# A streaming-encoder block on one core: rotation and decay masks moved from the chunk tiles into the input projection, through DRAM

## What is computed

```python
proj = x @ w_in                                   # one combined input projection
aq, ak = apply_rope(aq), apply_rope(ak)           # t1*c - t2*s, t2*c + t1*s
y_attn = banded_sink_attention(aq, ak, av, sinks) # chunks of 64 frames
g = cumsum(g)                                     # per chunk and head
decay = exp(where(tril, g[..., :, None] - g[..., None, :], -inf))
m_low = where(strict, einsum(k_beta, k) * decay, 0)
t_inv = solve(eye + m_low, eye)                   # then a scan over 16 chunks
o = (q * exp(g)) @ state + (q k^T * decay) @ v_new
```

## Time and profile before

| | us |
|---|---|
| median of 3 runs (lowest, highest) | 1432.07 (1429.08, 1433.17) |
| the profiled execution, its own time | 1435.67 |
| its span, first to last instruction | 1433.9 |
| input pairs, PE's first product to the first filler | 33.1 to 307.2 |
| chunk tiles, step -2 | 307.2 to 325.2 |
| chunk tiles, steps -1 to 7 | 325.2 to 620.2 |

### The profile page before, as it was taken

How to read it: one execution, slowest core, us unless ns; L and a number is a source line. 1 busy time by engine, 2 the same in 40 slices (tenths; PEclk the granted TensorE clock), 3 DMA queues, 4 the chain that set the end, 5 groups by cost and what they waited for, 6 DMA issues and landing times.

```text
span 1433.9 us, 22065 instructions
## 1 busy us (share of the span) xinstructions
PE 1392.7 (97%) x8430; PEld 1154.0 (80%) x8430; DVE 1024.1 (71%) x1860; ACT 600.7 (42%) x1300; POOL 257.4 (18%) x265
## 2 busy tenths in 40 slices
PE   9999999999999899999999999999999999999997
PEld 8788887877778778778888888888888888888885
DVE  7999863436888888754618798667665677777778
ACT  5555534321333333343202436554554544444540
POOL 4322222223332332514730000000000000000002
PEclk9999999999999999999999999999999999999998
DMA  6233322264244332123551234334444976555422
GB/s 209 89 117 118 117 105 102 105 197 107 77 119 106 84 105 66 62 105 132 176 206 59 88 133 158 134 143 160 162 161 144 347 235 182 167 166 183 126 73 117
DMA packets 114136, 195.01 MB, mean 136 GB/s; under 512 B 27696, under 2 KB 59632, under 8 KB 111728
## 3 DMA queue, kind: packets, MB, share of 16 engines
q1 hardware_dynamic: 105104, 174.21, 36.9%
q10 hardware_dynamic: 8928, 19.40, 3.5%
HBM read 135.84 MB, written 57.74 MB: 135 GB/s over the span
## 4 chain that ended last, share of the span: by engine, by line
PE 85%; DVE 11%; issue 1%; DMA 1%; ACT 1%; SPq 0%; ACTq 0%; DVEq 0%
PE ps L2498 6%; PE ps L2497 6%; PE ps L2496 6%; PE ps L2060 6%; PE ps L2479 6%; PE ps L2480 6%; PE ps L2481 6%; PE ps L2062 6%; PE ps L2061 6%; PE ps L2114 5%; PE ps L2000 4%; PE ps L2001 4%; PE ps L2002 4%; PE ps L2181 3%; PE ps L2373 2%; PE ps L2374 2%
## 5 line engine op out<-in xcount | busy, mean ns | idle before, releaser
L2497 PE MATMUL ps<-tlow,shi 128*128 128x512 f32 x416 | 162.0, 389 | 0.0
L2498 PE MATMUL ps<-thi,slow 128*128 128x512 f32 x416 | 162.0, 389 | 0.0
L2496 PE MATMUL ps<-thi,shi 128*128 128x512 f32 x416 | 162.0, 389 | 0.0
L886 POOL TENSOR_TENSOR zt<-zt,ln2gb 128x256 f32<-128x256 f32 x4 | 3.4, 852 | 691.6 <-ACT zt L1332 691.6
L896 ACT ACTIVATE thi<-b 128x512 fp32r<-128x512 f32 x104 | 65.5, 629 | 107.6 <-PE ps L2498 107.4
L1884 DVE TENSOR_TENSOR tlow<-b,thi 128x512 fp32r<-128x512 f32 x104 | 71.8, 691 | 52.7 <-ACT thi L896 52.6
L2497 PEld LDWEIGHTS ps<-tlow,shi 128*128 128x128 f32 x416 | 78.1, 188 | 16.3
L2496 PEld LDWEIGHTS ps<-thi,shi 128*128 128x128 f32 x416 | 78.1, 188 | 16.2
L2498 PEld LDWEIGHTS ps<-thi,slow 128*128 128x128 f32 x416 | 78.1, 188 | 16.1
L1877 DVE TENSOR_TENSOR slow<-sraw,shi 128x512 fp32r<-128x512 f32 x104 | 71.4, 687 | 21.6 <-ACT shi L896 21.1
L896 ACT ACTIVATE shi<-sraw 128x512 fp32r<-128x512 f32 x104 | 65.1, 626 | 32.8 <-DMA zt<-xpark 16.1
(11 more groups left out here) (444 smaller groups left out, 3940.5 us busy)
## 6 DMA issues: line engine op xcount, KB each, us to landing
raw<-in_wblk SPq DMA_DIRECT2D x55, 512.0 KB, 4.4
sraw<-hpark SPq DMA_DIRECT2D x104, 256.0 KB, 2.8
hpark<-hq SPq DMA_DIRECT2D x16, 1024.0 KB, 4.7
b<-in_wblk SPq DMA_DIRECT2D x64, 256.0 KB, 3.7
wraw<-in_wblk SPq DMA_DIRECT2D x30, 512.0 KB, 3.9
hpark<-hq SPq DMA_DIRECT2D x16, 768.0 KB, 5.0
park<-cb ACTq DMA_DIRECT2D x34, 256.0 KB, 2.5
park<-cacc ACTq DMA_DIRECT2D x12, 512.0 KB, 3.3
```

The costliest lines, as they stand in the source:

```text
L2496: mm(outp, shi[s][:, ts], thi[m][:, :], start=first, stop=False, skip_group_check=True)
L2497: mm(outp, shi[s][:, ts], tlow[m][:, :], start=False, stop=False, skip_group_check=True)
L2498: return mm(outp, slow[s][:, ts], thi[m][:, :], start=False, stop=final, skip_group_check=True)
```

## The change

- The rotation is done in the input pairs. Ten half rows (five blocks of `park` times two halves of 512 frames) pass one after the other through one buffer: ACT issues the loads (`rope_load`: one transfer of the block, four of the swapped quarters, at three of them a table), POOL does three operations of 128x512 (`rope`), SP stores the half row back. `rope_load(u)` waits for the store of `rope(u - 1)`. In the tiles SP loads the rotated values straight into `qb` and `kr`.
- The decays of all eight tiles are made in the input pairs from pair 8 on. Their rows go to DRAM (`gpark`); from pair 10 on ACT loads one tile's rows spread over 128 partitions (`dec_load`), DVE makes the arguments (`dec_args`), ACT the exponentials (`dec_exps`) and the store to `dpark`, again through one buffer. In each step SP loads the finished masks of a tile (`load_dec`). `a_grow`, `a_d`, `a_em`, `a_eg` and `a_exps` are gone; `a_trk` takes over the wait of `a_grow`.
- Six filler weight blocks are split by ACT (`split_hi`) and DVE (`split_lo`) instead of POOL.
- The orders of the steps are new on all engines, with 28 places for fillers; the number of fillers stays 384 (52 instead of 50 of them in step -2, 51 instead of 65 in step 7). Decay sums and rates move to pairs 7 to 9.

```diff
-    [0, 0, 6, 0, 1, 0, 0, 0, 0, 0, 0, 0, 0, 1, 0, 1, 0, 2, 2, 0, 0, 0, 13, 1, 2, 0, 0, 21, 0, 0, 0],
...
+    [7, 2, 0, 0, 0, 4, 6, 0, 0, 1, 1, 2, 0, 0, 0, 4, 0, 0, 0, 0, 0, 3, 0, 0, 22, 0, 0, 0],
...
+BEHIND = {-1: LATE + 2, 1: LATE + 3, 2: LATE + 4, 3: LATE + 5, 5: LATE + 6, 6: LATE + 7}
...
+        ROPE = [(0, 0), (1, 0), (2, 0), (0, 1), (1, 1), (2, 1), (3, 1), (4, 1), (3, 0), (4, 0)]
+        ROPE_TAB = [n for n, (_, h) in enumerate(ROPE) if n == 0 or ROPE[n - 1][1] != h]
+        ROPE0, DEC0 = 8, 10
+        ROPE_IN = [16 * (5 * (n + 1) + sum(m <= n for m in ROPE_TAB)) for n in range(len(ROPE))]
+        def rope_cols(n):
+            i, h = ROPE[n]
+            return B_Q + i, slice(PAD + h * HALF, PAD + (h + 1) * HALF)
...
+            def load_dec(t):
+                if t:
+                    sp.wait_ge(m_ok, 2 * t)
+                    sp.wait_ge(at_ok, t)
+                    sp.wait_ge(qegt_ok, t)
+                else:
+                    sp.wait_ge(dec_out, 16 * NT)
+                sp.dma_start(dec[:, :], dpark[t, :, :]).then_inc(dec_in, 16)
...
+                if t:
+                    sp.wait_ge(sc_mm, 2 * t)
+                else:
+                    sp.wait_ge(init_ok, 1)
+                    sp.wait_ge(rope_out, 16 * len(ROPE))
+                    sp.wait_ge(pad_out, 48)
+                for e, r in enumerate(chunks):
+                    for c in range(2):
+                        a = PAD + t * P + c * CH
+                        sp.dma_start(qb[r, c, :, r], park[B_Q:B_Q + N_Q, r, a:a + CH].rearrange("b p s -> p b s")).then_inc(bt_in, 16)
+                sp.dma_start(kr[:, :], park[B_K, :, t * P:t * P + 192]).then_inc(bt_in, 16)
...
+                for u in (2 * (n - ROPE0) - 3, 2 * (n - ROPE0) - 2):
+                    if 0 <= u < len(ROPE):
+                        sp.wait_ge(rope_ok, u + 1)
+                        b, sl = rope_cols(u)
+                        sp.dma_start(park[b, :, sl], rraw[:, :]).then_inc(rope_out, 16)
+                if n == DEC0:
+                    sp.wait_ge(g_eg, 1)
+                    sp.dma_start(gpark[:, :].rearrange("t (h s) -> (t h) s", h=NH), grow_[:, :]).then_inc(pad_out, 16)
             load_a(0, 0)
             load_dv(0)
-            load_ks(0, 0)
+            load_dec(0)
             load_w(LATE + 2, 1)
             load_w(LATE + 3, 0)
-            load_qk(0)
+            load_ks(0, 0)
             load_v(0)
             load_a(1, 1)
             load_dv(1)
             load_dz(0)
-            ahead = {0: LATE + 4, 1: LATE + 5, 2: LATE + 6, 4: LATE + 7, 5: B_BR}
+            load_dec(1)
+            load_qk(0)
+            ahead = {0: LATE + 4, 1: LATE + 5, 2: LATE + 6, 3: LATE + 7, 5: B_BR}
             for t in range(NT - 1):
-                load_qk(t + 1)
-                if t < NT - 2:
-                    load_dv(t + 2)
-                load_ks(t + 1, (t + 1) % 2)
                 if t < NT - 2:
                     load_a(t + 2, t % 2)
                 if t in ahead:
                     load_w(ahead[t], ahead[t] % 2)
+                if t < NT - 2:
+                    load_dec(t + 2)
+                if t < NT - 2:
+                    load_dv(t + 2)
+                load_qk(t + 1)
+                load_ks(t + 1, (t + 1) % 2)
+                load_v(t + 1)
                 load_dz(t + 1)
...
+            def rope(u):
+                pool.wait_ge(rope_in, ROPE_IN[u])
+                pool.tensor_tensor(rraw[:, :], rraw[:, :], rtab[:, 0, :], ALU.mult).then_inc(rope_mul, 1)
+                pool.tensor_tensor(rswp[:, :], rswp[:, :], rtab[:, 1, :], ALU.mult).then_inc(rope_mul, 1)
+                pool.wait_ge(rope_mul, 2 * u + 2)
+                pool.tensor_tensor(rraw[:, :], rraw[:, :], rswp[:, :], ALU.add).then_inc(rope_ok, 1)
             for n in range(N_IP):
+                u = 2 * (n - 1 - ROPE0)
+                if 0 <= u < len(ROPE):
+                    rope(u)
                 in_sums(n)
+                if 0 <= u < len(ROPE):
+                    rope(u + 1)
...
+            pool.wait_ge(w_ready, B_BR)
...
+            def rope_load(u):
+                if u == 0:
+                    for q in range(2):
+                        act.wait_ge(dn_out[q], 8 * N_DN)
+                else:
+                    act.wait_ge(rope_out, 16 * u)
+                b, sl = rope_cols(u)
+                for q in range(2):
+                    act.wait_ge(ub_out[q], 48 if ROPE[u][0] < 3 else 80)
+                if u in ROPE_TAB:
+                    act.dma_start(rtab[:, :, :], A["rope"][:, :, sl]).then_inc(rope_in, 16)
+                act.dma_start(rraw[:, :], park[b, :, sl]).then_inc(rope_in, 16)
+                for q in range(4):
+                    r = q ^ 1
+                    act.dma_start(rswp[32 * q:32 * q + 32, :], park[b, 32 * r:32 * r + 32, sl]).then_inc(rope_in, 16)
+            def dec_load(t):
+                if t == 0:
+                    act.wait_ge(pad_out, 48)
+                    act.wait_ge(vpark_out, 16)
+                else:
+                    act.wait_ge(dec_out, 16 * t)
+                act.dma_start(decp[:, 0:NH * P], gpark[t, :].partition_broadcast(P)).then_inc(dec_ld, 16)
+            def dec_exps(t):
+                row, lo_, up_ = decays(decp)
+                act.wait_ge(dec_arg, 2 * t + 1)
+                act.activation(lo_, lo_, ACT.Exp, scale=-1.0)
+                act.activation(up_, up_, ACT.Exp)
+                act.activation(row, row, ACT.Exp).then_inc(dec_arg, 1)
+                act.wait_ge(dec_arg, 2 * t + 2)
+                act.dma_start(dpark[t, :, :], decp[:, :]).then_inc(dec_out, 16)
...
+                if n > DEC0:
+                    dec_exps(2 * (n - DEC0) - 1)
...
                 in_snap(n, 0)
                 if ahead:
                     in_hi(n + 1, "A11", "A22", "A12")
+                if 0 <= 2 * (n - ROPE0) < len(ROPE):
+                    rope_load(2 * (n - ROPE0))
+                if n >= DEC0:
+                    dec_load(2 * (n - DEC0))
                 if conv:
                     silu_store(2 * n - 2)
                 in_snap(n, 1)
...
                 in_snap(n, 2)
+                if n >= DEC0:
+                    dec_exps(2 * (n - DEC0))
                 if ahead:
                     in_hi(n + 1, "S2", "S4")
+                if 0 <= 2 * (n - ROPE0) < len(ROPE):
+                    rope_load(2 * (n - ROPE0) + 1)
+                if n >= DEC0:
+                    dec_load(2 * (n - DEC0) + 1)
                 if conv:
                     silu_store(2 * n - 1)
                 if ahead:
                     in_hi(n + 1, "S3")
...
             in_snap(N_IP - 1, 3)
+            dec_exps(NT - 1)
             store_pair(N_IP - 1)
...
+            def split_hi(b):
+                act.wait_ge(w_raw_in[b % 2], 16 * (b // 2 + 1))
+                act.wait_ge(w_ready, b)
+                act.wait_ge(uni_mm, 2 * (b - 1))
+                cp(ring2h[b % 2][:, :, :], raw[b % 2][:, :].rearrange("p (k c) -> p k c", k=KT)).then_inc(w_hi, 1)
...
+            def dec_args(t):
+                row, lo_, up_ = decays(decp)
+                dve.wait_ge(dec_ld, 16 * t + 16)
+                for r in chunks:
+                    ins = tt(lo_[r, :, :], row[r, :, r], bc(G[r, t, G_CUM:G_CUM + NH], CH), ALU.subtract)
+                chain(ins)
+                chain(tt(up_, lo_, bh(msk(M_MU)), ALU.add))
+                tt(lo_, lo_, bh(msk(M_ML)), ALU.add).then_inc(dec_arg, 1)
...
             for n in range(N_IP - 1):
                 convs = 1 <= n <= N_DN // 2
-                if n == N_DN // 2 + 2:
-                    decay_rates()
                 if n:
                     combine_in(n - 1, 3)
+                if n > DEC0:
+                    dec_args(2 * (n - DEC0) - 1)
                 if convs:
                     conv(2 * n - 2)
                 in_lo(n + 1, "A11", "A22", "A12")
+                if n == N_DN // 2 + 1:
+                    decay_rates()
                 combine_in(n, 0)
+                if n == ROPE0 + 1:
+                    dve.wait_ge(g_dif, 1)
+                    chain(tt(G[:, :, G_NBEG:G_NBEG + NH], G[:, :, G_BETA:G_BETA + NH], G[:, :, G_EG:G_EG + NH], ALU.mult))
+                    dve.tensor_scalar(G[:, :, G_NBEG:G_NBEG + NH], G[:, :, G_NBEG:G_NBEG + NH], -1.0, None, ALU.mult).then_inc(g_all, 1)
                 in_lo(n + 1, "S1")
                 if convs:
                     conv(2 * n - 1)
+                if n >= DEC0:
+                    dec_args(2 * (n - DEC0))
                 combine_in(n, 1)
+                if n == ROPE0:
+                    decay_sums()
                 in_lo(n + 1, "S2", "S4")
                 combine_in(n, 2)
                 in_lo(n + 1, "S3")
             combine_in(N_IP - 2, 3)
...
-            def a_d(t, p):
-                dve.wait_ge(grow_mm, t + 1)
-                for r in chunks:
-                    ins = tt(dd[r, :, :], C1h[r, :, r], bc(gs[p][r, G_CUM:G_CUM + NH], CH), ALU.subtract)
```

(26 more changed lines are left out.)

261 lines of the change are left out of this document (112 added, 149 removed), and 18 rows, old and new, of the table FILLS.

## The result

The changed kernel takes **1454.6 us** (median of 4 runs, 1453.9 to 1455.7) against 1431.4 us of the kernel before in the same comparison: a ratio of 1.0164, 95% interval 1.0146 to 1.0181. It is slower by 23 us, where 9 us were forecast. The profiled execution took 1454.25 us with a span of 1452.4 us, 18.5 us over the span before; most of the difference between 23 and 18.5 us is that the profiled execution of the kernel before ran 4.3 us above its median here.

What follows compares the result with a forecast made beforehand. PE was taken as 97% busy, with DVE, stretched beside POOL, setting the pace at places in the tiles and PE tight in the pairs. Steps -22, pairs +28, step -2 +3 gave +9 us: 1441 us, range 1408 to 1460.

Steps and rivals of the forecast that it cites:

- Steps -1 to 7: In the tiles: 3 us from dropped `a_grow`, 13 idle, 6 clock, together -22 us, between -3 and -31.
- stretched DVE time: Steps -1 to 7: DVE's small operations are lengthened beside POOL's rotation, 25 to 35 us, which leaves with it.
- Idle time: Steps -1 to 7: PE idles 19.2 us, two thirds of it, 13 us, won back; steps 7 and -1 keep theirs.
- Rival B: Tiles: PE is near its floor and freed DVE time becomes idle, only -8 us there; 1455 us, chance 0.08.
- The rotation in the pairs: Pairs 8 to 12: even rotations delay the third snapshot; sixth product 3.3 us late, 5.2 us with the clock.
- this gate: Pairs 8 to 12: PE's sixth product waits for ACT's third snapshot, which the rotation delays through S1; 3.3 us late.
- The masks in the pairs: Pairs 10 to 13: mask work on ACT's queue delays rotation loads; 2.5 us each in pairs 11 and 12, 1 in 13.
- Just met: Odd mask from pair 10: done at T + 31.9 (T: pair start), in time for the next pair's fourth product.
- Step -2: Before the steps: the last masks are stored and loaded late, up to 4 us; +3 us, 0 to 7.
- C: Pairs: DVE's subtractions block POOL's rotation at each of its three operations, 10 us more; 1451 us, chance 0.05.
- D: Whole kernel: gains and costs meet within 4 us, nothing moves; 1432 us, chance 0.07.
- A: Whole kernel, faster: pairs cost only bare stalls, +14 us, tiles -28, step -2 +1; 1419 us, chance 0.39.

Runs made afterwards that it cites:

- e4: Kernel before, with POOL's rotation operations in the steps cut to one column (keys and queries not rotated): 1406.9 us against 1432.0.
- e2: Changed kernel without its masks: the three mask functions do nothing and stored data is loaded instead; the rotation stays: span 1426.1 us.
- e3: Changed kernel without rotations and masks; tile order, splits and loads of the steps stay: 1403.8 us against 1432.0 of the kernel before.
- e5: Changed kernel with ACT's third snapshot ahead of the rounding of S1 from pair 8 on: span 1454.3 us.
- e1: Changed kernel without its ten rotations (queries and keys unrotated), masks still made: span 1411.0 us.
- e9: Changed kernel with three moves around step -2: last pair stored before the last exponentials, keys squared earlier, buffers cleared earlier: span 1440.9 us.
- e6: Changed kernel with the odd mask's exponentials and store behind the next pair's first snapshot, not ahead of it: span 1455.0 us.
- e12: Changed kernel with rotation transfers issued by SP, even rotation between S4 and S3, snapshots ahead of POOL-dependent roundings, e9's moves: 1417.0 us, ratio 0.989.
- e13: e12 with the odd rotation's straight load ahead of the weights and the even mask made ahead of S1's rounding: 1406.1 us, ratio 0.9815.

## Why the prediction was off

**Steps -1 to 7, forecast -22 us, measured -34.5.** The reading was right: stretched DVE time (25 to 35 us forecast, 24.4 shown by e4, the splits left aside), `nmx` at 0.17 us, no wait on `osb`, the clock back from 0.97 to 0.99 (6 us forecast: 8.9 less 2.6 us). Idle time fell from 19.2 to 1.2 us, 18 for the 13 counted: steps 7 and -1 kept next to none. The rest, some 10 us by the same count, stands against 3 us for `a_grow`; e4, where nothing was dropped, also has PE 10.5 us less busy, 6 of them by the clock. The gain of 34.5 us lies beyond the bound of 31; the 4.3 us by which the profiled execution of the kernel before ran above its median may be part of it. Rival B (PE near its floor, 8 us) is refuted, and that its 1455 us is the measured time is luck: its tiles are off by 26 us one way and its pairs and step -2 by 24 the other.

**The rotation in the pairs, forecast +22.3 (5.7 + 1.3 + 4.9 + 5.2 + 5.2), measured +23.7 (e2 against e3).** The wait came at the sixth product, 3.70 us in pair 8 for 3.3 counted. POOL's S1 began at T + 16.0 in pairs 8 and 10; the working has its start at T + 14.3 and its end at T + 15.6. The sum is nearer than its terms, which is luck in part: by pair, e2 less e3 gives 5.4, -0.9, 6.9, 4.4 and 7.9 us. The working adds 1.9 us of lower clock behind each of these waits, and in pair 8 of the changed kernel there was none. And the reason was only half told: e5 removes this gate and gains nothing, since the two rotations form a ring that ACT steps into at several places.

**The masks in the pairs, forecast +6 (2.5, 2.5, 1), measured +4.3 alone and +22.8 on top of the rotation. This is the step that failed.** Its own clock can be checked in pair 10 (T = 236.49). The mask row's load was to be issued by T + 26.1, and was, at T + 26.7. Then the working took 2.4 us for the landing, from the nearest row; it took 5.5. It took 1.6 us for the arguments; they took 4.5, beside POOL. The exponentials and the issue took 1.7 us for 1.8. So the snapshot came at T + 38.5 and not at T + 31.9, 6.6 us late. "Just met" at the fourth product became a wait of 5.22 us, and 6.05 and 6.25 us in pairs 12 and 13, 17.5 us before any loss of clock. The landing was priced by a store in another stage, the arguments by operations with POOL idle; the change puts them beside 1 MB of weights, five loads and the rotation itself. What each costs is in e1 against the changed kernel: beside the weights alone the row of an odd mask lands after 4.0 to 4.2 us and the arguments take 1.8, beside the rotation too it is 5.5 to 6.6 and 4.5 to 5.2. The stretched arguments could be known from the very argument on the tiles, that DVE is stretched beside POOL, and from the 1.81 us for 0.69 that the working itself read in pair 11. The same effect was counted as a gain where POOL left and at nothing where it arrived.

**Step -2, forecast +3 (0 to 7), measured +8.4.** Some 3 us of it go with the masks (e2), as forecast. The other 5 are there without masks and rotation too (e3, 23.3 us for 18.0): they are the new order of ACT and DVE, which the working put at nothing and e9 mends.

**Rivals.** C, POOL blocked by DVE for 10 us, is refuted: the ten rotations took 39.7 us on POOL in the pairs, 1.31, 1.38 and 1.29 us a piece against 1.26 alone, 2 us more in all. The blocking cut the other way, at the mask arguments. That C's 1451 us is near the measured time is luck as well. D, nothing moves, is refuted by the 23 us. A was nearer in the tiles (-28) and wrong in the pairs.

Against the profiled execution's own time the forecast was 1445 us and 1454.25 came: pairs 18.7 us too low, step -2 5.4 too low, steps 12.5 too high, and 2.1 us gained at the ends that were not counted.

**Still open.** The three odd masks of pairs 11 to 13 are 15.3 us later beside the rotation than without it, and the interaction is 18.5 us; that the first makes the second, one for one, is not shown, since no run took the slow landing without the stretched arguments, and the masks push the rotation's loads back in turn. How much of the 8.3 us in the steps is the order and how much the dropped work was not tried.

## What to carry to other kernels

Work moved off a crowded stage is paid for in the stage that takes it, at the prices of that stage: a landing time or an operation's length read where little else ran is too low (2.4 us became 5.5, 1.6 became 4.5), and two chains that share engines can cost more than their sum: the masks, 4.3 us by themselves, cost 22.8 us beside the rotation. In an in-order queue look for every instruction that waits on another chain, not for the one that shows in the stall: moving one thing past it moves the stall to the next (e5, e6), and what helped was to take the transfers to a queue on which nothing urgent stands behind, together with the snapshots ahead of every rounding that waits (e12), and then the order of issue and of the masks (e13); these moves were not tried one by one. When an engine's small operations are several times longer than their twins, test it as e4 does: shrink the other engine's work and leave everything else.

## What was not expected of the hardware

- Cutting POOL's rotation to one column in the kernel before, and nothing else, is worth 25 us of 1432: DVE operations of 0.17 us last until the end of POOL's current one, up to 1.19 us.
- A straight load of 256 KB took 2.5 and 2.6 us to land where no weights were under way (at 208, 219 and 244 us in the changed kernel) and 4.8 to 7.2 us right behind two loads of 512 KB (five times in e12). A mask row, also 256 KB, took 3.0 to 3.5 us in the quiet places of e1 and 5.5 to 6.6 us behind weights and rotation. The transfers of the changed kernel from 262 to 328 us:

```profile
decp<-gpark ACTq DMA_DIRECT2D x5, 256.0 KB, 5.5
...
raw<-in_wblk SPq DMA_DIRECT2D x4, 512.0 KB, 6.2
```

- A good third of the stalls came again as longer matmuls: 34.2 us of added waits in the pairs brought 12.5 us. But not every wait did it: behind 3.70 us in pair 8 nothing was lost, behind 3.35 us in pair 9 six matmuls ran at the lower level (1.3 us).
